# End of the experts: the last down weights in column halves, squares between them, the residual kept in its own order

## The chip, the cores and the metric

The kernel runs on one core of a Trainium2 chip. The metric is the device time of one execution in microseconds (us), the median of several runs. In the program and the profile TensorE is PE (its weight loads PEld), VectorE is DVE, ScalarE is ACT, GpSimd is POOL and the engine that issues most transfers is SP.

## What is computed

Two transformer blocks, one after the other, on 256 tokens of width 1024. The first block is a mixer (attention and convolution) and then a mixture of 32 experts with top 2 of one group of 8; the second is a block with an LRU, attention and an MLP. The change sits at the seam of the two: the end of the experts, the norm of their sum, and the first norm of the second block.

```python
    a = jnp.einsum('nd,edf->nef', t, w_gate)
    b = jnp.einsum('nd,edf->nef', t, w_up)
    hid = jax.nn.silu(a) * b * combine[:, :, None]
    routed = jnp.einsum('nef,efd->nd', hid, w_down)
    shared = (jax.nn.silu(t @ w_sh_gate) * (t @ w_sh_up)) @ w_sh_down
    return (routed + shared).reshape(bsz, slen, d)
...
        h = h + rms_norm(ffn, post_ffn_norm[l])
...
        h = rmsnorm(x, norm_mix_g[l])
        proj = h @ w_in[l]
```

`rms_norm(x, g)` divides x by the root of the mean of its squares over the 1024 columns (plus 1e-6) and multiplies by g. All is float32.

## The kernel before

Each engine has its own program, written by hand in order; semaphores join them. The weights stream through a ring of slots of 1 MB each (`slot(s)`, 12 in the experts, 8 in the second block). The 32 experts are worked in 8 quads of 4 (`q` from 0 to 7). A quad uses slots 0 to 3 for w_gate, 4 to 7 for w_up, 8 to 11 for w_down. SP issues the loads of the even slots and POOL those of the odd ones (`expert_slabs`), each as soon as the quad before has used the slot.

On PE a quad is: 64 passes of gate (`gate_or_up`, L2162), 64 of up (L2162), two transposes of the hidden rows (`turn_hidden`, L2169), down (`down`, L2176: 128 rows by 1024 columns into banks 2 and 3), and combine (L2183): the rows, copied from PSUM to `yrow` by ACT (columns 0 to 511, L889) and DVE (512 to 1023, L1516), are multiplied by the transposed selection `sel_T` and added to the tokens' sums in banks 4 to 7. A token tile t (128 tokens, two of them) has banks 4+2t and 5+2t. In the last quad combine of quad 6 comes between gate and up, followed by 16 filler matmuls (`keep_busy`, L2076).

After the last combine: PE takes a branch on `overflow` (L2288, L2289) around a long block that serves experts with over 32 tokens and that is not entered here, then issues 6 fillers, waits for the first tile of the sum (`h_ffn`), issues 8 more, and transposes the normed tiles (`turn_rows`, L2087) ahead of the first unit of the second block (L1843 to L1845, 24 passes for each unit). ACT and DVE do for each token tile: square with a sum (L930), root (L933), reciprocal (L1604), sum times root times gain from PSUM (L1605), plus the residual (L1609), square (L937), root, reciprocal (L1614), scale (L1615); then the high and low parts XH and XL of the transposed tiles. The residual is `h_tok`, which holds its columns in another order: `by_row` reads a row with steps of 128 elements, and `in_order` names the same columns in natural order. Between these, ACT splits the first units of new weights into a high part (`high2`, L648) and DVE into a low part (`low2`, L1133). ACT loads the table of roots ahead of the first square (`square_root_ahead`, L656).

Of the kernel before, what the change touches and what calls it, by code (L numbers as in the profile page):

```python
# [12 lines left out]
ALU = mybir.AluOpType  # L13
# [108 lines left out]
def build(nc, A, out):  # L122

    ctx = ExitStack()
    with ctx:
# [7 lines left out]
        def const(name):  # L133
# [5 lines left out]
                    "overflow_known", "lambda_abs", "ple_root"),  # L139
            scalar=("meta_std", "router_high", "mix_std", "group_exp", "pair_exp", "lambda_exp"),  # L140
            tensor=("angles", "kpe_swapped", "mix_sums", "routed", "ranks", "expert_totals"))
# [112 lines left out]
        gain_ffn = ar(0, D)  # L254

# [161 lines left out]

        def expert_slabs(queue, parity):

            for q in range(QUADS):  # L420
                for s in range(parity, RING, 2):
# [13 lines left out]
        def _(sp):  # L435
# [33 lines left out]
            expert_slabs(sp, 0)  # L469

# [45 lines left out]
        def _(pool):  # L516
# [70 lines left out]
            pool.dma_start(gain_mix, broadcast(A["post_mix_norm"][0])).then_inc(ev("gain_mix_loaded"), 16)  # L587
# [7 lines left out]
            pool.dma_start(gain_ffn, broadcast(A["post_ffn_norm"][0])).then_inc(ev("gain_ffn_loaded"), 16)  # L595
# [23 lines left out]
            for gain, name in ((gain_mlp, "norm_mlp_g_2"), (gain_ple, "norm_ple_g_2"), (gain_final, "norm_final_g_2")):  # L619
                v = A[name] if name == "norm_final_g_2" else A[name][0]  # L620
                pool.dma_start(gain, broadcast(v)).then_inc(ev("gains_loaded"), 16)
# [5 lines left out]
        def _(act):  # L627
# [186 lines left out]
            junk2 = junk.rearrange("p (b n) -> p b n", b=2)  # L814
# [69 lines left out]
            def rows_of(q):  # L884

                act.wait_ge(ev("expert_slab_used"), (q + 1) * RING)
# [15 lines left out]
            for q in range(1, QUADS):  # L902
# [3 lines left out]
                silu_of(q)  # L906
                if q % 2 == 0:
                    turned_weights(o)
                rows_of(q)
                if q == 4:  # L910
                    act.wait_ge(*mark("lambda_abs"))
                    s.activation(small_lru[:, 2 * DC:3 * DC], small_lru[:, DC:2 * DC], ACT.Exp)\
                        .then_inc(ev("scalar_mark"), 1)
            act.wait_ge(*mark("overflow_known"))
            more = act.value_load(overflow[0:1, 0:1], min_val=0, max_val=1)
            with act.If(more > 0):
# [7 lines left out]
                act.wait_ge(*by_tensor("combined", (ROUNDS - 1) * QUADS - 1))  # L924

            high2(0)
            square_root_ahead(1)
            for t in range(TT):
                act.wait_ge(ev("ffn_summed"), t + 1)
                s.activation(junk2, ps[:, 4 + 2 * t:6 + 2 * t, :], ACT.Square, accum_out=st(6, t))\  # L930
                    .then_inc(ev("tok_square"), 1)
                act.wait_ge(ev("tok_square"), 2 * TT + t + 1)
                s.activation(st(7, t), st(6, t), ACT.Sqrt, scale=1.0 / D, bias=EPS).then_inc(ev("tok_std"), 1)  # L933
            high2(1)
            for t in range(TT):
# [4 lines left out]
                if t == 0:  # L940
# [1623 lines left out]
```

## Time and profile before

| | us |
|---|---|
| median of 3 runs | 899.44 (898.21 to 900.03) |
| the profiled execution, its own time | 899.61 |
| its span, first to last instruction | 897.9 |
| PE busy in the span | 811.9 |
| DVE busy | 485.1 |
| ACT busy | 381.3 |

The span is what the trace shows; 1.7 us of the execution's time lie around it. Times of rows are counted from the span's start. The experts end and the second block begins near 385 to 401 us.

### The profile page before, as it was taken

The page shows a single profiled execution, that of the slowest core. Times are in us where ns is not written, and L with a number is a line of the kernel's source. Part 1 is how long each engine was busy: PE and PEld are TensorE (multiplying, and loading weights), DVE is VectorE, ACT ScalarE, POOL GpSimd, SP SyncE. Part 2 cuts the span into 40 slices and gives each one's busy share as a digit, 9 for nine tenths or more (in the row PEclk, how much of TensorE's full clock was granted, in tenths as well). Part 3 has the DMA queues.
Part 4 walks back from the last instruction along what each step waited for, and adds up shares of the span by engine and source line. Part 5 has one row for each costly group of instructions (what it writes and reads, how often), then busy time and mean ns, then how long its engine had stood idle before and what let it go on. Part 6 is the DMA issues. An engine that isn't in the chain of part 4 may idle for free.

```text
span 897.9 us, 13410 instructions
## 1 busy us (share of the span) xinstructions
PE 811.9 (90%) x5491; PEld 642.5 (72%) x5491; DVE 485.1 (54%) x799; ACT 381.3 (42%) x643; POOL 48.4 (5%) x114
## 2 busy tenths in 40 slices
PE   6989999997877676879999998999999999999995
PEld 5977879764444332449989885558888999999974
DVE  6786648411110030064936585776666666666675
ACT  5564558310000100065456845655444544444454
POOL 5000030101010001000000000000000000000000
PEclk9998999999897888899999998999999999999998
DMA  9951154899999999996418554127555555555101
GB/s 281 376 194 47 48 217 182 346 380 423 420 420 422 420 421 421 411 344 210 141 63 313 189 197 142 48 97 255 165 166 177 188 188 187 189 186 195 49 1 47
DMA packets 76974, 205.81 MB, mean 229 GB/s; under 512 B 5720, under 2 KB 48896, under 8 KB 64624
## 3 DMA queue, kind: packets, MB, share of 16 engines
q1 hardware_dynamic: 68430, 150.44, 47.2%
q0 software_dynamic: 8480, 54.49, 15.0%
q8 instruction: 45, 0.74, 0.3%
q14 instruction: 17, 0.14, 0.0%
q10 hardware_dynamic: 2, 0.00, 0.0%
HBM read 203.87 MB, written 1.05 MB: 228 GB/s over the span
## 4 chain that ended last, share of the span: by engine, by line
PE 71%; DMA 16%; DVE 6%; ACT 4%; issue 2%; SPq 0%; POOL 0%; ACTq 0%; DVEq 0%
DMA big<-in_w_up 13%; PE ps L2049 10%; PE ps L2050 10%; PE ps L2051 9%; PE ps L1843 9%; PE ps L1845 8%; PE ps L1844 8%; PE ps L2162 5%; DMA big<-in_w_down 3%; PE ps L2141 1%; PE ps L2176 1%; DVE WL L1133 1%; PE ps L2396 1%; ACT WH L648 1%; PE ps L2333 1%
## 5 line engine op out<-in xcount | busy, mean ns | idle before, releaser
L1133 DVE TENSOR_TENSOR WL<-big,WH 128x1024 fp32r<-128x1024 f32 x154 | 186.6, 1222 | 105.9 <-ACT WH L648 105.0
L648 ACT ACTIVATE WH<-big 128x1024 fp32r<-128x1024 f32 x154 | 160.5, 1054 | 70.5 <-PE ps L2051 70.0
L1843 PE MATMUL ps<-XH,WH 128*128 128x256 f32 (+1 forms) x640 | 187.6, 293 | 2.1 <-DVE XL L1198 0.9
L1845 PE MATMUL ps<-XH,WL 128*128 128x256 f32 (+1 forms) x640 | 183.3, 286 | 0.0
L1844 PE MATMUL ps<-XL,WH 128*128 128x256 f32 (+1 forms) x640 | 183.3, 286 | 0.0
L1843 PEld LDWEIGHTS ps<-XH,WH 128*128 128x128 f32 x640 | 123.9, 194 | 7.8 <-issue 5.0
L1844 PEld LDWEIGHTS ps<-XL,WH 128*128 128x128 f32 x640 | 124.0, 194 | 0.8
L1845 PEld LDWEIGHTS ps<-XH,WL 128*128 128x128 f32 x640 | 123.8, 193 | 0.0
L2162 PE MATMUL ps<-big 128*32 128x256 f32 x1024 | 77.6, 470 | 40.8 <-DMA big<-in_w_gate 25.2
L2049 PE MATMUL ps<-WH,XH 128*128 128x512 f32 x240 | 98.0, 408 | 1.8 <-ACT big L986 1.0
L2162 PEld LDWEIGHTS ps<-big 128*32 128x32 f32 x1024 | 42.5, 134 | 76.9 <-issue 66.3
L2050 PE MATMUL ps<-WH,XL 128*128 128x512 f32 x240 | 94.1, 392 | 0.0
L2051 PE MATMUL ps<-WL,XH 128*128 128x512 f32 x240 | 94.1, 392 | 0.0
L1504 DVE TENSOR_TENSOR big<-big,ps 128x256 f32<-128x256 f32 x8 | 3.4, 421 | 124.9 <-ACT big L882 124.8
L2049 PE MATMUL ps<-WH,HH 128*128 128x512 f32 x152 | 59.9, 394 | 0.6 <-DVE HL L1798 0.6
L2050 PE MATMUL ps<-WH,HL 128*128 128x512 f32 x152 | 59.4, 391 | 0.0
L2051 PE MATMUL ps<-WL,HH 128*128 128x512 f32 x152 | 59.2, 390 | 0.0
L2049 PEld LDWEIGHTS ps<-WH,XH 128*128 128x128 f32 x240 | 45.3, 189 | 13.5 <-issue 2.8
L1125 DVE TENSOR_TENSOR WL<-big,WH 128x1024 fp32r<-128x1024 f32 (+1 forms) x39 | 40.5, 1044 | 25.6 <-ACT WH L639 25.4
L2051 PEld LDWEIGHTS ps<-WL,XH 128*128 128x128 f32 x240 | 45.3, 189 | 9.8
L2050 PEld LDWEIGHTS ps<-WH,XL 128*128 128x128 f32 x240 | 45.4, 189 | 7.8
L1075 ACT ACTIVATE HH<-big 128x256 fp32r<-128x256 f32 x32 | 13.4, 418 | 76.1 <-DVE big L1795 76.1
(397 smaller groups left out, 1085.2 us busy)
## 6 DMA issues: line engine op xcount, KB each, us to landing
big<-in_w_in SPq DMA_DIRECT2D x35, 1024.0 KB, 9.4
big<-in_w_gate SPq DMA_DIRECT2D x16, 1024.0 KB, 14.6
big<-in_w_up SPq DMA_DIRECT2D x16, 1024.0 KB, 15.0
big<-in_w_gate POOLq DMA_DIRECT2D x16, 1024.0 KB, 18.7
big<-in_w_up POOLq DMA_DIRECT2D x16, 1024.0 KB, 19.2
big<-in_w_down SPq DMA_DIRECT2D x16, 1024.0 KB, 15.4
big<-in_w_down POOLq DMA_DIRECT2D x16, 1024.0 KB, 19.4
big<-in_w_mlp_up SPq DMA_DIRECT2D x16, 1024.0 KB, 5.4
```

The source lines that it names most:

```text
L648: s.activation(dst, src, ACT.Copy).then_inc(ev("unit_high"), 1)
L1075: s.activation(HH[:, f % 2, :], zx[:, f % 2, :], ACT.Copy).then_inc(ev("relu_high"), 1)
L1125: v.tensor_tensor(dst, src, h.bitcast(F32), ALU.subtract).then_inc(ev("unit_split"), 1)
L1133: v.tensor_tensor(dst, src, h.bitcast(F32), ALU.subtract).then_inc(ev("unit_split"), 1)
L1843: mm(o, h, rh, start=first, stop=False, skip_group_check=skip)
L1844: mm(o, h, rl, start=False, stop=False, skip_group_check=skip)
L1845: return mm(o, l, rh, start=False, stop=last, skip_group_check=skip)
L2049: mm(o, h, WH[:, b, w], start=first, stop=False, skip_group_check=skip)
L2050: mm(o, l, WH[:, b, w], start=False, stop=False, skip_group_check=skip)
L2051: return mm(o, h, WL[:, b, w], start=False, stop=last, skip_group_check=skip)
L2141: last = mm(o, h_tok[:, t, c * P:(c + 1) * P], sel[:, b, t, first:first + width].bitcast(F32), start=t == 0, stop=t == TT - 1)
L2162: last = mm(ps[j * CAP:(j + 1) * CAP, 1, up * FF:(up + 1) * FF], x(c)[:, j * CAP:(j + 1) * CAP], slot(first_slot + j)[:, c * FF:(c + 1) * FF],
```

## The change

It does six things, all at the end of the last quad. The four last w_down slabs are loaded in two column halves each (0 to 511, 512 to 1023); SP loads slots 8, 9 and 10 (all first halves, then all second), POOL slot 11, and SP starts the second block's weights only once POOL's second half is in. PE does down for the first half into bank 2, combine for it, then down for the second half in two quarters into banks 3 and 0, and combine for it. ACT squares the first half's sums while the second goes on. The residual, scaled and in natural order, is copied by ACT to slot 7 ahead of the last rows (so the load of the second block's slab 7 waits for `h_ffn`). DVE multiplies the sums by the gain (`weighted`) ahead of the root, so that one operation after the root adds the residual. The root's table is loaded after the last silu, and the splits of the first units of new weights are placed later.

```diff
+        weighted = lambda t: ar((1 + t) * D, D)
+        residual = lambda t: slot(RING2 - 1)[:, t * D:(t + 1) * D]
...
+        def last_down_halves(queue, slots):
+            for n in range(2):
+                for s in slots:
+                    queue.wait_ge(ev("expert_slab_used"), (QUADS - 2) * RING + s + 1)
...
+                    cols = slice(n * 512, (n + 1) * 512)
+                    queue.dma_start(slot(s).rearrange("p (c n) -> p c n", c=2)[:, :, cols], w[:, :, cols])\
+                        .then_inc(*last_half(n, s))
...
             expert_slabs(sp, 0)
+            last_down_halves(sp, (8, 9, 10))
+            sp.wait_ge(ev("last_half_by_pool"), 16)
...
             for m in range(RING2):
                 sp.wait_ge(ev("expert_slab_used"), RING * (QUADS - 1) + m + 1)
+                if m == RING2 - 1:
+                    sp.wait_ge(ev("h_ffn"), TT)
                 second_slab(m)
...
             expert_slabs(pool, 1)
+            last_down_halves(pool, (11,))
# ACT
                 silu_of(q)
+                if q == QUADS - 1:
+                    square_root_ahead(1)
...
+                if q == QUADS - 1:
+                    for t in range(TT):
+                        ins = s.activation(in_order(residual(t)), by_row(h_tok[:, t, :]), ACT.Copy, scale=st(4, t))
+                    ins.then_inc(ev("scalar_mark"), 1)
                 rows_of(q)
...
+            act.wait_ge(*mark("half_combined"))
+            square_part(0, 0, half_square[:, 0:1])
+            square_part(0, 1, half_square[:, 1:2]).then_inc(ev("scalar_mark"), 1)
+            act.wait_ge(ev("expert_slab_used"), QUADS * RING)
+            s.activation(yrow[:, 768:D], ps[:, 0, 0:256], ACT.Copy).then_inc(ev("rows_by_scalar"), 1)
...
-            high2(0)
-            square_root_ahead(1)
             for t in range(TT):
                 act.wait_ge(ev("ffn_summed"), t + 1)
-                s.activation(junk2, ps[:, 4 + 2 * t:6 + 2 * t, :], ACT.Square, accum_out=st(6, t))\
+                square_part(1, t, st(6, t)).then_inc(ev("tok_square"), 1)
...
+            high2(0)
             high2(1)
# DVE
-            low2(0)
...
+            for t in range(TT):
+                dve.wait_ge(ev("tok_square"), 2 * TT + t + 1)
+                chain(scale_part(1, t))
                 dve.wait_ge(ev("tok_std"), 2 * TT + t + 1)
                 chain(v.reciprocal(st(8, t), st(7, t)))
...
-                v.scalar_tensor_tensor(out=in_order(ffn_tmp[:, t, :]), in0=by_row(h_tok[:, t, :]), scalar=st(4, t),
-                                       in1=in_order(ffn_tmp[:, t, :]), op0=ALU.mult, op1=ALU.add)\
-                    .then_inc(ev("h_ffn"), 1)
+                v.scalar_tensor_tensor(out=ffn_tmp[:, t, :], in0=weighted(t), scalar=st(8, t), in1=residual(t),
+                                       op0=ALU.mult, op1=ALU.add).then_inc(ev("h_ffn"), 1)
...
                 v.tensor_scalar(h2n[:, t, :], ffn_tmp[:, t, :], st(11, t), None, ALU.mult).then_inc(ev("tok_normed"), 1)
-            low2(1)
+                low2(t)
# PE
+            last_down(2, 0, 512).then_inc(ev("tensor_mark"), 1)
             pe.wait_ge(ev("rows_by_scalar"), QUADS)
+            for t in range(TT):
+                last = combine(sel_T[:, 1, 1], t, (0,))
+            last.then_inc(ev("tensor_mark"), 1)
+            pe.wait_ge(ev("last_halves"), 16 * (QUAD - 1))
+            pe.wait_ge(ev("last_half_by_pool"), 16)
+            last_down(3, 512, 768)
+            last_down(0, 768, D).then_inc(ev("expert_slab_used"), QUAD)
+            pe.wait_ge(ev("rows_by_scalar"), QUADS + 1)
             pe.wait_ge(ev("rows_by_vector"), QUADS)
             for t in range(TT):
-                combine(sel_T[:, 1, 1], t).then_inc(ev("ffn_summed"), 1)
+                combine(sel_T[:, 1, 1], t, (1,)).then_inc(ev("ffn_summed"), 1)
```

On PE, from the up matmuls of the last quad to the branch and past it, the order before is (`ps` is PSUM, `big` the arena with slots and rows):

```order
L2162 MATMUL ps<-big 32x256 x32
L2169 MATMUL ps<-ident,big 128x128 x2
L2176 MATMUL ps<-big 32x512 x16
L2183 MATMUL ps<-big 128x512 x4
L2288 TENSOR_LOAD overflow
L2288 ISA x2
L2289 COMPARE_AND_BRANCH
```

and in the changed kernel, same place:

```order
L2225 MATMUL ps<-big 32x256 x32
L2232 MATMUL ps<-ident,big 128x128 x2
L2352 MATMUL ps<-big 32x512 x8
L2246 MATMUL ps<-big 128x512 x2
L2352 MATMUL ps<-big 32x256 x16
L2246 MATMUL ps<-big 128x512 x2
L2374 TENSOR_LOAD overflow
L2374 ISA x2
L2375 COMPARE_AND_BRANCH
```

Down and combine are cut in two and interleaved; the branch stays behind the last combine, and behind the skipped block the 14 fillers and 16 transposes stay as they were.

On ACT, from the last silu (first row) to the branch, the order of the changed kernel is (L940 copies the residual, L916 and L956 the rows, L950 squares):

```order
L909 ACTIVATE big<-ps 128x256
L684 ACT_TABLE_LOAD
L684 ACTIVATE warm<-ones 1x1
L940 ACTIVATE big<-hT,stat 128x1024 x2
L916 ACTIVATE big<-ps 128x512
L950 ACTIVATE big<-ps 128x512 x2
L956 ACTIVATE big<-ps 128x256
L958 TENSOR_LOAD overflow
```

Before, the copy of the rows (L889) followed the silu (L882) directly and was the last before the branch; the table load and the two copies of 128x1024 now stand between them, ahead of the rows for which PE waits.

On DVE, behind the skipped block, the order before is:

```order
L1133 TENSOR_TENSOR WL<-big,WH 128x1024
L1604 RECIPROCAL stat<-stat 128x1
L1605 SCALAR_TENSOR_TENSOR big<-ps,stat,big 128x1024
L1609 SCALAR_TENSOR_TENSOR big<-hT,stat,big 128x1024
L1604 RECIPROCAL stat<-stat 128x1
L1605 SCALAR_TENSOR_TENSOR big<-ps,stat,big 128x1024
L1609 SCALAR_TENSOR_TENSOR big<-hT,stat,big 128x1024
L1614 RECIPROCAL stat<-stat 128x1
L1615 TENSOR_SCALAR big<-big,stat 128x1024
L1614 RECIPROCAL stat<-stat 128x1
L1615 TENSOR_SCALAR big<-big,stat 128x1024
L1133 TENSOR_TENSOR WL<-big,WH 128x1024
```

and in the changed kernel (L1568 is sum times gain for one half, L1673 the addition of the residual, L1180 `low2`):

```order
L1568 TENSOR_TENSOR big<-ps,big 128x512
L1672 RECIPROCAL stat<-stat 128x1
L1673 SCALAR_TENSOR_TENSOR big<-big,stat 128x1024
L1568 TENSOR_TENSOR big<-ps,big 128x512
L1672 RECIPROCAL stat<-stat 128x1
L1673 SCALAR_TENSOR_TENSOR big<-big,stat 128x1024
L1677 RECIPROCAL stat<-stat 128x1
L1678 TENSOR_SCALAR big<-big,stat 128x1024
L1180 TENSOR_TENSOR WL<-big,WH 128x1024
L1677 RECIPROCAL stat<-stat 128x1
L1678 TENSOR_SCALAR big<-big,stat 128x1024
L1180 TENSOR_TENSOR WL<-big,WH 128x1024
```

The two operations of 128x1024 for each tile are one of 128x512 and one of 128x1024, and the first split of weights has moved from ahead of both tiles to between the two scalings.

## Rows read from the trace of the kernel before

**Rows 1.** The chain that ended last, 350 to 425 us: start, duration, what.

```profile
357.21 23.88 DMA big<-in_w_down
381.23 3.67 PE ps L2176 x32
```

**Rows 2.** The same chain, 384 to 402 us; ACTq is ACT's sequencer.

```profile
385.68 0.05 ACTq L916
...
387.00 1.28 ACT L656
...
394.74 2.07 DVE big L1609
...
396.83 1.16 ACT big L937 x2
...
398.45 0.75 DVE big L1615
399.20 1.13 DVE WL L1133
...
400.88 0.36 PE ps L1843
```

**Rows 3.** Timeline of PE, 366 to 420 us: start, busy, operation, count, idle before.

```profile
371.25 4.22 PE L2076 MATMUL ps<-router 128*128 128x512 f32 x16
...
375.40 3.66 PE L2162 MATMUL ps<-big 128*32 128x256 f32 x64
...
381.23 3.64 PE L2176 MATMUL ps<-big 128*32 128x512 f32 x32 [0.64 <-DMA big<-in_w_down]
...
385.76 3.67 PE L2183 MATMUL ps<-big 128*128 128x512 f32 x8 [0.90 <-DVE big L1516]
...
393.37 5.06 PE L2076 MATMUL ps<-router 128*128 128x512 f32 x14 [3.93 <-issue]
...
398.26 2.09 PE L2087 MATMUL ps<-ident,big 128*128 128x128 f32 x16
```

**Rows 4.** Source line L2289: PE's branch (ns min/median/max, first and last start).

```profile
L2289 PEldq COMPARE_BRANCH  x1: 6646/6646/6646, 386.7 to 386.7; - x1
```

**Rows 5.** Windows: length, busy (count) of PE, PEld, DVE, ACT, POOL; clock; DMA.

```profile
393.00:396.00 3.00, 2.63 (x9) 2.13 (x10) 2.93 (x4) 2.31 (x4) 0.00 (x0) 0.78 1.10 348
396.00:398.00 2.00, 2.00 (x7) 1.52 (x6) 1.62 (x3) 1.15 (x2) 0.00 (x0) 0.50 1.10 350
...
410.00:420.00 10.00, 10.00 (x86) 10.00 (x85) 3.73 (x4) 6.20 (x9) 0.00 (x0) 1.00 0.67 215
```

**Rows 6.** Groups of ACT and of DVE by form: busy us, mean ns of one, idle before.

```profile
L648 ACT ACTIVATE WH<-big 128x1024 fp32r<-128x1024 f32 x154 | 160.5, 1054 | 70.5 <-PE ps L2051 70.0 <-issue 0.4
...
L889 ACT ACTIVATE big<-ps 128x512 f32<-128x512 f32 x8 | 4.8, 597 | 65.9 <-PE ps L2176 65.9
L844 ACT ACTIVATE hT<-big,stat 128x1024 f32<-128x1024 f32 x2 | 4.1, 2180 | 0.0
...
L1609 DVE SCALAR_TENSOR_TENSOR big<-hT,stat,big 128x1024 f32<-128x1024 f32 x2 | 4.0, 2018 | 0.1
...
L1370 DVE SCALAR_TENSOR_TENSOR big<-big,stat,hT 128x1024 f32<-128x1024 f32 x2 | 2.6, 1285 | 0.1
```

**Rows 7.** Timeline of ACT, 379 to 403 us.

```profile
379.13 0.38 ACT L882 ACTIVATE big<-ps 128x256 f32<-128x256 f32 x1 [22.10 <-PE ps L2162]
...
389.30 0.18 ACT L930 ACTIVATION_READ_ACCUMULATOR big<-ps 128x1 f32 x1
```

**Rows 8.** POOL's last w_down transfer, issued at 357.2 us: KB, us to landing.

```profile
big<-in_w_down POOLq DMA_DIRECT2D x1, 1024.0 KB, 23.9
```

**Rows 9.** DMA queues, 376 to 378 us (q0 POOL's, q1 SP's): packets, MB, share.

```profile
q0 software_dynamic: 98, 0.69, 83.1%
q1 hardware_dynamic: 92, 0.11, 15.4%
```

More of the change, by code:

```diff
@@ L416, in expert_slab, with last_half @@
             queue.dma_start(dst, src).then_inc(ev(expert_in(s)), 16)
+        def last_half(n, s):
+            if s == RING - 1:
+                return ev("last_half_by_pool" if n else expert_in(s)), 16
+            return ev("last_halves" if n else expert_in(s) if s % 2 == 0 else "last_slot_9"), 16
+        def last_down_halves(queue, slots):
+            for n in range(2):
+                for s in slots:
+                    queue.wait_ge(ev("expert_slab_used"), (QUADS - 2) * RING + s + 1)
+                    w = A["w_down"][0][bass.ds((QUADS - 1) * QUAD + s % QUAD, 1)].rearrange("e (p c) n -> p (e c) n", p=P)
+                    cols = slice(n * 512, (n + 1) * 512)
+                    queue.dma_start(slot(s).rearrange("p (c n) -> p c n", c=2)[:, :, cols], w[:, :, cols])\
+                        .then_inc(*last_half(n, s))
         def expert_slabs(queue, parity):
             for q in range(QUADS):
-                for s in range(parity, RING, 2):
+                for s in range(parity, RING if q < QUADS - 1 else 2 * QUAD, 2):
                     if q == 0:
@@ L620, in _ @@
                 v = A[name] if name == "norm_final_g_2" else A[name][0]
-                pool.dma_start(gain, broadcast(v)).then_inc(ev("gains_loaded"), 16)
+                pool.dma_start(gain, broadcast(v)).then_inc(ev("rows_loaded"), 16)
         @block.scalar
@@ L1568, in _ @@
                     softplus_of_lambda()
+            dve.wait_ge(*loaded("gain_ffn"))
+            for t in range(TT):
+                ins = scale_part(0, t)
+            chain(ins)
             dve.wait_ge(*mark("overflow_known"))
@@ L2179, in down, with combine @@
                 return last
-            def combine(weights, t):
-                for n in range(2):
+            def combine(weights, t, halves_=(0, 1)):
+                for n in halves_:
                     last = mm(ps[:, 4 + 2 * t + n, :], weights[:, t * P:(t + 1) * P], yrow[:, n * 512:(n + 1) * 512],
@@ L2280, in _, with last_down @@
                     pe.wait_ge(ev("sel_T_ready"), o + 1)
-                wait_slots(q, 2 * QUAD)
-                down(2 * QUAD).then_inc(ev("expert_slab_used"), QUAD)
-            pe.wait_ge(ev("rows_by_scalar"), QUADS)
+                if q < QUADS - 1:
+                    wait_slots(q, 2 * QUAD)
+                    down(2 * QUAD).then_inc(ev("expert_slab_used"), QUAD)
+            def last_down(bank, a, b):
+                for f in range(2):
+                    for j in range(QUAD):
+                        last = mm(ps[j * CAP:(j + 1) * CAP, bank, 0:b - a], hidT[:, f, j * CAP:(j + 1) * CAP],
+                                  slot(2 * QUAD + j)[:, f * D + a:f * D + b],
+                                  start=f == 0, stop=f == 1, skip_group_check=True)
+                return last
+            for s in (8, 10, 11):
+                pe.wait_ge(*slab_e(QUADS - 1, s))
+            pe.wait_ge(ev("last_slot_9"), 16)
+            last_down(2, 0, 512).then_inc(ev("tensor_mark"), 1)
+            pe.wait_ge(ev("rows_by_scalar"), QUADS)
+            for t in range(TT):
+                last = combine(sel_T[:, 1, 1], t, (0,))
[5 more added lines that the diff above has]
+            pe.wait_ge(ev("rows_by_scalar"), QUADS + 1)
             pe.wait_ge(ev("rows_by_vector"), QUADS)
             for t in range(TT):
-                combine(sel_T[:, 1, 1], t).then_inc(ev("ffn_summed"), 1)
+                combine(sel_T[:, 1, 1], t, (1,)).then_inc(ev("ffn_summed"), 1)
             more = pe.value_load(overflow[0:1, 0:1], min_val=0, max_val=1)
```

56 lines of the change are left out of this document (37 added, 19 removed).

## The prediction

> **What bounds the kernel now.** I read the page first, then the chain of waits around the seam, then the timelines of PE, ACT and DVE there. The chain says that the last w_down slab holds the end of the experts: 23.88 us on a transfer, down from 381.23 [rows 1], and then a ladder of ACT and DVE steps up to 400.88, where the first unit of the second block starts on PE [rows 2]. From there PE is busy without a break, 10.00 of the 10 us from 410 [rows 5], so I let a shift of that start pass to the end one for one. So the question is only: when does the first unit start?
>
> Two paths reach it, and the chain shows one of them. The other is PE's own program. After the last combine PE sits idle for 3.93 us ("issue"), then runs 14 fillers to 398.26, and only then transposes [rows 3]. The idle time is its branch: it starts at 386.7, 0.9 us behind the start of combine, and holds for 6.65 us [rows 4], where ACT's branch on the same word takes 0.05 [rows 2]. The transposes of the first tile begin as soon as the fillers end. So the ladder of ACT and DVE and the ladder of PE arrive together: from the start of the transposes, 398.26, PE alone would have needed some 2.35 us to the first unit (8 transposes, half of the 2.09 us of the 16, then a pair, ACT's high and DVE's low part at 0.4 to 0.5 each), so 400.6 against 400.88. **PE has 0.3 us of slack there.** What makes its last combine end later makes the kernel slower, whatever is saved on ACT and DVE.
>
> **The change, step by step.**
>
> Loads. The total is the same; SP's queue has 3 MB and POOL's 1 MB in place of 2 and 2. Before, the last slab landed 23.9 us behind its issue, at 381.1 [rows 1, 8]. Where POOL's large packets met SP's small ones of w_in, POOL moved 0.69 MB and SP 0.11 in 2 us at about the same number of packets [rows 9]: the queues take turns by packet. Halves have pieces of 2 KB in place of 8, so SP's first halves advance slowly while POOL finishes its up slab, then evenly. I put the first halves at 379 to 381 and the second ones at 382.5 to 384.5 (an estimate: the 381.1 of before with the same bytes, plus the gain row's 0.5 MB, which now moves in between, at 350 GB/s [rows 5], and up to two more for smaller pieces). The hidden rows are ready at 381.2 as before, since up starts at 375.40 behind the fillers [rows 3], so first halves cost nothing up to 381.2 and, by the next step, up to some 383 unseen. The second halves are wanted at 387.5. w_in then follows: its first slab, 1 MB at those 350 GB/s, lands 3 us later, near 387; it is split at 393, as shown below. Cost of all this: 0; cover 3 us and more.
>
> Down, first half: 16 of 32 passes, half of 3.67 us, ends at 383.2 [rows 1].
>
> ACT's way to the rows. Silu ends at 379.5 [rows 7], table load 1.28 [rows 2] and the warm-up operation to 380.9, then two copies of the residual with steps of 128 elements. No row has ACT *reading* so. Below: the plain copy, 1.05 us (L648). Above: ACT *writing* such a pattern, 2.18 (L844). DVE reading this very pattern takes 2.02 against 1.29 for the same operation on plain rows (L1609, L1370) [rows 6]. Both nearest rows pay for the pattern, so I take 2.1 each: ACT is free at 385.1. At 1.05 it is free at 383.0, and the rows start at 383.2. The Trainium skill (SBUF — State Buffer, section "Door 1: The DMA port swizzle", its note on cachelines) says that fp32 strides over 4 elements leave full bandwidth; by it too the copies cost double and the sum is the one below, but no run here shows an ACT read of that kind.
>
> The rows' copy, 0.60 [rows 6], and 0.1 to PE: combine of the first half starts at 385.8, just where the whole combine started before (385.76 [rows 3]). So nothing of the overlap is left: PE idles 2.6 us between the halves, and now still has the second down ahead.
>
> PE from 385.8: four passes of combine 1.8 (half of 3.67); second down, 32 passes of 256 columns in place of 16 of 512, 1.8 (half of the 3.66 of 64 such passes [rows 3]), to where its readers start 2.0, so 389.6; DVE's copy of 256 columns 0.4 (an estimate, two thirds of ACT's 0.60 for 512), 0.1 to PE, so combine starts at 390.1; four passes and the drain 2.0: **the last combine ends at 392.1, against 389.43 before** (385.76 plus 3.67), +2.7. The passes cost in sum what they did. But behind 385.8 there stood one combine, and now stand half a combine, half a down, a copy and the other half combine.
>
> ACT and DVE meanwhile. Squares of the first half (two times 0.6 and 0.18 [rows 6, 7]) fit under the second down. From the sum of tile 0 at 391.3: square of 512 columns and its sum 0.8; gain times sum on DVE 0.7; reciprocal and gap 0.2; one addition 1.29 on plain rows: tile 0 at 394.3. Tile 1: another 2.3, at 396.6, where L1609 ended at 396.8 before [rows 2]. All that DVE saves (0.7 a tile by plain rows, 0.6 by a half product, the table load) is spent on starting 3 us later. Then both splits on ACT (2.1) lie ahead of the square of tile 0, so squares end at 396.6 and 398.0 and root 0.2 behind each; DVE scales tile 0 to 397.8, splits a unit (1.13), scales tile 1 to 400.0, splits again to 401.1, low part: first unit at 401.8 by this path (399.20 to 400.88 is the same last stretch [rows 2]). So this path alone gives +0.9. With quick residual copies it would be 399.9, so -1.0.
>
> PE's branch. Its 6.65 us can hang on two things. If it waits for the last matmul (idle 3.93 behind it [rows 3]), the fillers start at 392.1 + 3.9 = 396.0, +2.7. If it is a fixed time from where it is reached (0.9 behind the start of combine, 390.1 + 0.9 + 6.65), they start at 397.7, +4.3. The Trainium skill (Runtime: NRT & Kernel Launch, section "Instruction fetch mechanics") says that a taken branch whose target is outside the two pages at hand stalls for a fetch; the 6.65 us agree with that, and by it a target within those pages would make the short branch of the rivals below. I take the first, as the two halves of combine leave less queued work behind which a fixed wait could hide, and it is the smaller claim; the second stays in the range.
>
> Fillers. From their start to the first transpose went 4.9 us (393.37 to 398.26), with the granted clock at 0.78 and then 0.50, which is 1.2 GHz [rows 3, 5]. At the full 2.4 GHz 14 take 3.7, by the 16 at 371.25 in 4.22 [rows 3]. PE is idle before them as long as it was, so I keep 4.9: transposes from 400.9, first unit 2.35 later. Bounds -1.4 (no drop) and +1.5 (half clock for all).
>
> **Sum.** +2.7 on the last combine, minus the 0.3 of slack: first unit at 403.3 in place of 400.88, **+2.4 us**. 899.61 for this profile would be 902.0; on the median, 0.17 below it, 901.8. A difference under 0.2% (1.8 us) can't be told from none.
>
> **Rivals.**
> - Branch of fixed length: +4.1, 903.5. For it: the branch is reached ahead of the last passes. Against: nothing in the trace says what it waits for.
> - One more drop of the clock, in the new idle stretch 383.2 to 385.8 or over all fillers: +1.5 to 1.7 on the forecast, 903.4. For it: an idle stretch of 3.9 us was followed by a drop; the new one is 2.6 us, so open.
> - Quick residual copies (1.05 each): rows at 383.2, all 1.9 earlier, +0.5, 899.9. Decides from a copy under some 1.15 us; at 1.6 each half of it.
> - Not slower, by a short branch: if it costs PE what it costs ACT, fillers start right behind the last combine and PE's path is no bound; then the path of ACT and DVE stands, +0.9 with slow copies (900.3) and -1.0 with quick ones (898.4). It decides once PE sits idle behind the last combine for 3.3 us or less in place of 3.93 (that is within 0.2%), and in full at 2.4. Against: the skipped block is the same and PE's code ahead of it grew by only 16 passes.
> - The halves don't overlap at all because the transfers are late: from 383.2 on each us costs one. Little speaks for it.
>
> **How the numbers follow.** Forecast 0.40 (901.8, own range 900.6 to 903.2), fixed branch 0.22, extra clock drop 0.13, quick copies 0.15, short branch 0.08, late loads or others 0.02. Slower by over 0.2%: most of the first three, 0.65. Within: quick copies, short branch with slow copies and the low edge of the forecast, 0.28. Faster: short branch and quick copies together with a clock that stays up, or something that I don't see, 0.07. The range 899.6 to 904.6 leaves out about one in ten on either side.
>
> **What would show it.** In the changed profile: the two residual copies at 2.0 to 2.2 us each and the copy of the first rows behind them at 385; PE idle 2 to 3 us between first down and first combine; last combine ending near 392; a branch row and the fillers near 396 (397.7 for the rival); transposes at 400 or later with no wait for the normed tile; first unit at 403. I am wrong if the fillers start before 394.5, if the copies are near 1 us, or if the transposes wait for DVE.

## The result and the profile after

The changed kernel takes 902.91 us (median of 14 runs, 899.6 to 906.87) against 898.18 for the kernel before (14 runs, 897.64 to 900.03): ratio 1.0054, 95% interval 1.004 to 1.0067. It is slower by about 4.7 us. The profiled execution took 901.96, its span is 900.2.

The chain that ended last in the changed kernel, around the seam (start, duration, what):

```profile
378.43 1.28 ACT L684
...
379.93 3.94 ACT big L940 x2
383.87 0.49 ACT big L916
384.40 1.98 PE ps L2246 x4
...
390.84 5.59 issue
396.43 5.15 PE ps L2139 x14
...
402.71 0.48 ACT XH L991
```

In [rows 2] ACT and DVE filled the chain up to the first unit. Here they fill it only ahead of the first combine, where PE waits for the table load and the two residual copies. From 384.40 on the chain is PE's own, but for DVE's copy of the last rows (0.44) and a step each of ACT and DVE ahead of the first unit, and its largest piece is idle time. PE's timeline for the same stretch (start, busy, operation, count, idle before and its releaser), which answers to [rows 3]:

```profile
380.02 1.92 PE L2352 MATMUL ps<-big 128*32 128x512 f32 x16 [0.52 <-DVE big L1556]
384.40 1.98 PE L2246 MATMUL ps<-big 128*128 128x512 f32 x4 [2.46 <-ACT big L916]
386.32 1.93 PE L2352 MATMUL ps<-big 128*32 128x256 f32 x32
388.89 1.96 PE L2246 MATMUL ps<-big 128*128 128x512 f32 x4 [0.64 <-DVE big L1564]
396.43 5.15 PE L2139 MATMUL ps<-router 128*128 128x512 f32 x14 [5.59 <-issue]
401.42 1.91 PE L2150 MATMUL ps<-ident,big 128*128 128x128 f32 x16
403.85 0.36 PE L1906 MATMUL ps<-XH,WH 128*128 128x256 f32 x1 [0.52 <-DVE XL L1682]
```

The first down waits for the hidden rows (L1556), not for a transfer. The last combine ends at 390.84 and the transposes need no wait for a normed tile. PE's branch, which answers to [rows 4], and the two residual copies (ns min/median/max, then first and last start):

```profile
L2375 PEldq COMPARE_BRANCH  x1: 6602/6602/6602, 389.8 to 389.8; - x1
L940 ACT ACTIVATE big<-hT,stat x2: 1996/2065/2134, 379.8 to 381.9; 128x1024 f32<-128x1024 f32 x2
```

And the last rows of DVE and of ACT on the other path, by their timelines (L1180 is DVE's last split, the other two are the low and high parts of the transposed tiles):

```profile
398.67 1.22 DVE L1180 TENSOR_TENSOR WL<-big,WH 128x1024 fp32r<-128x1024 f32 x1
403.22 3.23 DVE L1682 SCALAR_TENSOR_TENSOR XL<-ps,vec,XH 128x256 fp32r<-128x256 f32 x8 [3.33 <-ACT XH L991]
402.71 3.03 ACT L991 ACTIVATE XH<-ps,vec 128x256 fp32r<-128x256 f32 x8 [4.45 <-PE ps L2150]
```

DVE is done with everything at 399.9 and sits idle for 3.33 us, ACT for 4.45. The steps that were made shorter on them now end in front of a PE that comes late.

**A gauge.** The start of the first down wanders between profiles, 379 to 385 us, and PE waits 5.4 to 7.6 us for the last quad's gate weights in all of them; the stretch from the first unit to the end is 497.0 us before and 496.4 after. So I compare the stretch from the start of the last quad's down to the first unit, cut at three points of PE's timeline: A from down to the start of the last group of combine, B from there to the fillers, C from the fillers to the transposes, D from the transposes to the first unit. What happens ahead of this down, the gauge doesn't see.

| kernel | A | B | C | D | sum |
|---|---|---|---|---|---|
| before | 4.53 | 7.61 | 4.89 | 2.62 | 19.65 |
| changed | 8.87 | 7.54 | 4.99 | 2.43 | 23.83 |
| e1 | 4.55 | 3.10 | 8.86 | 3.17 | 19.68 |
| e2 | 10.52 | 1.39 | 6.54 | 3.61 | 22.06 |
| e3 | 8.86 | 7.53 | 2.73 | 2.99 | 22.11 |
| e4 | 7.13 | 7.56 | 5.80 | 2.43 | 22.92 |
| e5 | 6.23 | 7.63 | 4.85 | 2.64 | 21.35 |
| e6 | 5.97 | 7.55 | 4.90 | 2.70 | 21.12 |
| e7 | 8.98 | 7.56 | 5.02 | 2.42 | 23.98 |
| e8 | 7.13 | 1.39 | 7.98 | 3.23 | 19.73 |
| e9 | 8.76 | 7.71 | 4.87 | 2.42 | 23.76 |
| e10 | 4.45 | 7.57 | 4.91 | 2.70 | 19.63 |
| e11 | 9.01 | 1.39 | 6.54 | 3.61 | 20.55 |
| e12 | 7.13 | 1.39 | 6.53 | 3.62 | 18.67 |

The change adds 4.2 us, all of it in A. The table also shows at once what B is: 7.5 to 7.7 wherever the branch stands behind combine, whether the group of combine ahead of it has 8 passes (3.67 to 3.70 us: before, e5, e6, e10) or 4 (1.96: changed, e3, e4, e7, e9). It is 0.9 to the branch and 6.6 in it. The changed kernel, e7 and e9 have the same order of work behind down and lie at 23.76 to 23.98, so a difference under 0.2 says nothing here.

### The profile page after: what moved, and what is told of

Its sections match the earlier page's. It is cut to its first block, busy times and chain, and to the rows that moved or that the text cites. A ratio compares the mean times of both kernels' runs of the same rounds, so it can differ in the third digit from the quotient of the medians.

```text
span 900.2 us, 13463 instructions
## 1 busy us (share of the span) xinstructions
PE 808.0 (90%) x5507; PEld 640.7 (71%) x5507; DVE 483.5 (54%) x802; ACT 386.3 (43%) x650; POOL 48.8 (5%) x114
## 4 chain that ended last, share of the span: by engine, by line
PE 72%; DMA 15%; DVE 5%; ACT 4%; issue 3%; SPq 0%; POOL 0%; ACTq 0%; DVEq 0%
DMA big<-in_w_gate 15%; PE ps L2112 10%; PE ps L2113 9%; PE ps L2114 9%; PE ps L1906 9%; PE ps L1907 8%; PE ps L1908 8%; PE ps L2225 5%; PE ps L2139 2%; PE ps L2204 1%; DVE WL L1180 1%; PE ps L2246 1%; PE ps L2482 1%; PE ps L2419 1%; PE ps L2468 1%
## 5 line engine op out<-in xcount | busy, mean ns | idle before, releaser
L1180 DVE TENSOR_TENSOR WL<-big,WH 128x1024 fp32r<-128x1024 f32 x154 | 186.6, 1222 | 104.4 <-ACT WH L676 103.5
L2225 PE MATMUL ps<-big 128*32 128x256 f32 x1024 | 74.7, 456 | 43.7 <-DMA big<-in_w_gate 28.3
```

The lines of the kernel that those rows point to most:

```text
L1180: v.tensor_tensor(dst, src, h.bitcast(F32), ALU.subtract).then_inc(ev("unit_split"), 1)
L2225: last = mm(ps[j * CAP:(j + 1) * CAP, 1, up * FF:(up + 1) * FF], x(c)[:, j * CAP:(j + 1) * CAP], slot(first_slot + j)[:, c * FF:(c + 1) * FF],
```

## Experiments

The expectations name three theories of what makes the changed kernel slower: theory 1 (T1), PE's own path, with a later last combine, then a branch of fixed length, then 14 fillers; theory 2 (T2), the ladder of ACT and DVE; theory 3 (T3), the loads. Each run has its own median of the kernel before, taken beside it.

**e1: the kernel before, PE's branch moved ahead of the last quad.** The code of the last quad stands twice, once in the block that is skipped and once behind it, so that the jump is over before the quad's first matmul (row of its branch: 6.05 us from 357.3, while PE waits for gate weights).

```diff
+            for q in range(1, QUADS - 1):
+                quad_of(q)
...
             with pe.If(more > 0):
+                end_of_experts()
...
+            with pe.If(more < 1):
+                end_of_experts()
```

> The kernel before, with PE's branch around the overflow block taken ahead of the last quad, where PE waits for w_gate anyway (the last quad's code stands in both arms). Theory 1 (PE's own path sets the first unit of the second block: last combine, then a branch of a fixed 6.6 us from where it is reached, then 14 fillers): before, that path had 0.3 us of slack, so taking the branch out of it gains nothing more than that: 898.2 less 0 to 0.5. Theory 2 (the ladder of ACT and DVE sets it): the same, 898.2. Both: the idle time of 3.9 us behind the last combine is gone, and PE waits for the normed tile instead.

Measured: 899.37 us (12 runs, 897.04 to 902.8) against 898.83, ratio 1.001 (0.9997 to 1.0024). PE's timeline:

```profile
392.33 1.95 PE L2076 MATMUL ps<-router 128*128 128x512 f32 x6
396.85 3.29 PE L2076 MATMUL ps<-router 128*128 128x512 f32 x8 [2.57 <-DVE big L1609]
401.19 1.09 PE L2087 MATMUL ps<-ident,big 128*128 128x128 f32 x8 [1.04 <-DVE big L1615]
```

The idle time behind combine is gone and nothing is gained: PE now waits for DVE at each step. The ladder alone takes 19.68, the kernel before 19.65; PE's path alone, with the ladder shortened, takes 19.63 (e10). In the kernel before, the two paths met, closer than the gauge can tell.

**e2: the changed kernel with the same edit.** The wrapper is e1's, around the last quad with its halves.

```diff
             with pe.If(more > 0):
+                end_of_experts()
...
+            with pe.If(more < 1):
+                end_of_experts()
```

> The changed kernel with the same early branch. Theory 1: the fillers start right behind the last combine (391 in place of 396.4), the transposes wait for DVE, first unit at about 400.5 in place of 403.9: -3.3, 899.6 on the median, and the wide scatter of the changed kernel (899.6 to 906.9) shrinks, since PE is no longer idle for 5.6 us. Theory 2: no change, 902.9. Theory 3 (the transfers or the held-back weights are what costs): no change, 902.9.

Measured: 901.97 us (11 runs, 900.63 to 904.03), ratio 1.0035 (1.0018 to 1.0051), 22.06 us in the stretch. Theory 1 had expected 899.6. B fell from 7.5 to 1.4, but A grew by 1.65. PE's timeline, and the windows (length, busy and count of PE, PEld, DVE, ACT, POOL, then clock, DMA):

```profile
386.05 2.56 PE L2246 MATMUL ps<-big 128*128 128x512 f32 x4 [2.46 <-ACT big L916]
388.54 2.99 PE L2358 MATMUL ps<-big 128*32 128x256 f32 x32
392.18 1.96 PE L2246 MATMUL ps<-big 128*128 128x512 f32 x4 [0.65 <-DVE big L1564]
...
400.11 1.09 PE L2150 MATMUL ps<-ident,big 128*128 128x128 f32 x8 [0.88 <-DVE big L1678]
```

```profile
383.70:387.30 3.60, 1.25 (x3) 0.68 (x4) 0.00 (x0) 2.29 (x2) 0.00 (x0) 1.00 1.10 349
387.30:390.70 3.40, 3.40 (x26) 1.02 (x28) 0.17 (x1) 1.26 (x4) 0.00 (x0) 0.50 1.10 348
```

Behind the idle stretch ahead of the first combine the granted clock stood at 0.50, 1.2 GHz, for 3.4 us, and combine and the second down took 2.56 and 2.99 in place of 1.98 and 1.93. Without that (e11) the stretch is 20.55. So within the stretch the branch was worth 3.3 us to the changed kernel (23.83 to 20.55; 3.4 from e7, which has the same fillers in the gap) and nothing to the kernel before.

The early branch has a price of its own ahead of the stretch. In the chains of the changed kernel and of e12, the last w_gate slab that PE waits for:

```profile
337.36 23.53 DMA big<-in_w_gate
```

```profile
336.65 24.91 DMA big<-in_w_gate
```

In the five profiles with an early branch (e1, e2, e8, e11, e12) this transfer takes 24.2 to 24.9 us, in eight with a late one 23.0 to 23.6 (the chain of the kernel before doesn't show it). From the start of quad 6's down to its combine, behind the last quad's gate, it is 16.1 to 16.4 us against 15.3 to 15.9, on average 0.7 more. Why the transfer takes longer, no run shows. The medians agree with it without proving it: e1, level with the kernel before in the stretch, lies 0.5 us above it, with no difference still inside the interval.

**e3: the changed kernel with 6 fillers in place of 14.**

```diff
             pe.wait_ge(ev("h_ffn"), 1)
-            keep_busy(8, 0)
             turn_rows(h2n, 1)
```

> The changed kernel with 6 fillers in place of 14 behind the branch. Theory 1: the transposes come 8 fillers earlier, 3.4 us at the half clock, of which DVE's path (first unit not before 400.5) lets 2.5 to 3.3 count: about 900.2; less if the missing fillers keep the clock at 1.2 GHz into the first units. Theories 2 and 3: no change.

Measured: 900.92 us (12 runs, 898.81 to 906.4), ratio 1.0031 (1.0009 to 1.0052), 22.11 us in the stretch; 900.2 was expected.

```profile
397.50 2.93 PE L2139 MATMUL ps<-router 128*128 128x512 f32 x6 [5.57 <-issue]
400.23 2.47 PE L2150 MATMUL ps<-ident,big 128*128 128x128 f32 x16
```

Fewer fillers bring the first unit forward by 1.7 us. They save 2.3 in C; 0.6 went back in D, in slower transposes and the pair behind them. Fillers lie on the path that sets the end, as T1 says; by T2, dropping them would have gained nothing. The medians (902.91 and 900.92, against 898.18 and 898.83 before) go the same way, with intervals that overlap.

**e4: the residual copied without its reordering** (it leaves out the reordering, so the residual's columns are mixed).

```diff
-                        ins = s.activation(in_order(residual(t)), by_row(h_tok[:, t, :]), ACT.Copy, scale=st(4, t))
+                        ins = s.activation(residual(t), h_tok[:, t, :], ACT.Copy, scale=st(4, t))
```

> The changed kernel with the residual copied by ACT without the change of order (it leaves out the reordering, so the values are others). The copies should take 1.05 us each in place of 2.0. Theory 1: first rows, both combines, the branch and all behind them come 1.7 to 1.9 us earlier: 901.1. Theory 2: the same 1.8 through the ladder. Theory 3: nothing.

Measured: 901.48 us (9 runs, 899.84 to 906.03), ratio 1.0043 (1.0024 to 1.0062), 22.92 in the stretch.

```profile
381.76 1.98 PE L2246 MATMUL ps<-big 128*128 128x512 f32 x4 [0.72 <-ACT big L916]
...
393.81 5.96 PE L2139 MATMUL ps<-router 128*128 128x512 f32 x14 [5.61 <-issue]
```

The first combine starts 2.64 us behind down in place of 4.38, so the pattern costs 1.7 us on PE's path; the two copies took 1.13 us each. Of that 0.8 was lost again over the fillers (C 5.80 in place of 4.99), which ran at half clock almost to their end (granted 0.50 from 394 to 398 us, 0.71 over the next two).

**e5: the kernel before with the new loads alone.** PE does down as a whole and waits for all halves.

```diff
             expert_slabs(sp, 0)
+            last_down_halves(sp, (8, 9, 10))
+            sp.wait_ge(ev("last_half_by_pool"), 16)
...
+                    pe.wait_ge(ev("last_halves"), 16 * (QUAD - 1))
+                    pe.wait_ge(ev("last_half_by_pool"), 16)
                 down(2 * QUAD).then_inc(ev("expert_slab_used"), QUAD)
```

> The kernel before with nothing but the loads of the change: last w_down slabs in column halves, three on SP and one on POOL, the second block's weights held until POOL's second half is in; PE waits for all of them and does down whole. Theory 1 (PE's path behind the first down costs the time): 898.8 within 0.2%, since down waits for the hidden rows and the slabs land within a microsecond or two of them. Theory 3 (the loads cost it): 902 or more, with first down later than 1 us behind the hidden rows.

Measured: 901.69 us (5 runs, 901.02 to 904.16) against 898.49, ratio 1.0047 (1.0033 to 1.0061). Not what I expected.

```profile
381.34 5.34 PE L2195 MATMUL ps<-big 128*32 128x512 f32 x32 [3.21 <-DMA big<-in_w_down]
387.57 3.67 PE L2202 MATMUL ps<-big 128*128 128x512 f32 x8 [0.90 <-DVE big L1535]
```

PE waits for the last half 2.7 us longer than for the hidden rows (3.21 of idle time, where the changed kernel has 0.52), and behind it down ran at half clock for most of its length (granted 0.50 from 382 to 384 us; 5.34 in place of 3.64). The gauge begins behind that wait and shows only the second part, 1.7. New loads do cost something, then, in a kernel that wants all halves at once. Whether the changed kernel does, e9 tells.

**e6: the changed kernel with down and combine whole again on PE** (new loads kept).

```diff
-            last_down(2, 0, 512).then_inc(ev("tensor_mark"), 1)
-            pe.wait_ge(ev("rows_by_scalar"), QUADS)
-            for t in range(TT):
-                last = combine(sel_T[:, 1, 1], t, (0,))
-            last.then_inc(ev("tensor_mark"), 1)
             pe.wait_ge(ev("last_halves"), 16 * (QUAD - 1))
             pe.wait_ge(ev("last_half_by_pool"), 16)
+            last_down(2, 0, 512).then_inc(ev("tensor_mark"), 1)
...
+            for t in range(TT):
+                last = combine(sel_T[:, 1, 1], t, (0,))
```

> The changed kernel with down and combine whole on PE (both halves of down, then the rows, then combine of all columns; ACT squares the first half's sums behind it), all else as changed. From the start of the last down: combine ends at +8.7 us (before +8.2, changed +10.8), branch of 6.6 from +5.8, fillers at +12.4 (before +12.1, changed +16.4), first unit at +20.0 (before 19.7, changed 23.8). Theory 1: some 3.8 us below the changed kernel, 899.2, the same as before. Theory 2 (ladder) and 3 (loads): 902 to 903 as changed.

Measured: 901.75 us (9 runs, 899.2 to 903.96), ratio 1.0029 (1.0012 to 1.0047), 21.12 us in the stretch. Theory 1 had expected 899.2 and 20.0 in the stretch. Something else confounds it: down took 5.35 us behind 2.99 of waiting for w_down, as in e5. It tells nothing of the halves alone; e10 repeats it with the old loads.

**e7: the changed kernel with 10 fillers in the gap ahead of the first combine.**

```diff
             last_down(2, 0, 512).then_inc(ev("tensor_mark"), 1)
+            keep_busy(10, 1)
             pe.wait_ge(ev("rows_by_scalar"), QUADS)
```

> The changed kernel with 10 fillers on PE in the 2.5 us in which it waits for the first rows. If a drop of the clock in that gap, as seen in the early-branch run at 387 to 391, makes the upper part of the changed kernel's scatter, then runs of 904 to 907 become rare and the median falls by 0 to 1.5 us: 901.5 to 902.9. If not, the same scatter and median. The branch and the order are untouched, so theory 1 has it stay above 901.

Measured: 902.14 us (5 runs, 900.87 to 903.36), ratio 1.0043 (1.003 to 1.0056), 23.98 us in the stretch. The fillers (2.60 us) all but fit into the wait of 2.46 and cost 0.1. The runs lie closer together (900.87 to 903.36) than the changed kernel's 899.6 to 906.87, but five runs don't settle that.

**e8: early branch, residual copied a quad earlier, first splits ahead of the second squares.** The residual goes to the arena's first rows at q = 6, when ACT waits for gate weights anyway; the gain row gives way to it and is loaded later, and the weighted sums move to slot 7.

```diff
-        residual = lambda t: slot(RING2 - 1)[:, t * D:(t + 1) * D]
+        residual = lambda t: ar(t * D, D)
...
+                rows_of(q)
+                if q == QUADS - 2:
...
-                rows_of(q)
...
+            high2(0)
             act.wait_ge(*mark("half_mean"))
...
+            low2(0)
             dve.wait_ge(*mark("residual_kept"))
```

> The changed kernel with three edits: PE's branch ahead of the last quad, the residual copied in quad 6 into a buffer that is free by then, and the first split of new weights ahead of the second half's squares (ACT and DVE idle there). Theory 1: first rows 2.1 us behind the start of down, last combine ends at +9.1, fillers at full clock behind it, then the ladder of ACT and DVE is the bound: first unit at +18.3 where before has 19.7, so 897.4, 0.15% under the kernel before. Theory 3: 902.

Measured: 898.46 us (12 runs, 897.25 to 903.73) against 898.49, ratio 1.0005 (0.9985 to 1.0024), 19.73 us in the stretch. The slowdown is gone, though 897.4 was expected. The splits cost: ahead of the second group of fillers PE sits idle for 2.67 us, where e12, without them, has 1.60.

```profile
393.72 3.52 PE L2142 MATMUL ps<-router 128*128 128x512 f32 x8 [2.67 <-DVE big L1675]
```

**e9: the changed kernel with the old loads** (whole slabs, POOL and SP two each).

```diff
-                for s in range(parity, RING if q < QUADS - 1 else 2 * QUAD, 2):
+                for s in range(parity, RING, 2):
...
-            last_down_halves(sp, (8, 9, 10))
-            sp.wait_ge(ev("last_half_by_pool"), 16)
```

> The changed kernel with the loads of before (whole w_down slabs, two on SP and two on POOL, the second block's weights not held); PE's halves and all else as changed. Theory 1 (PE's path behind the first down): the first down waits for whole slabs, 0 to 0.5 us later than changed, and the stretch from first down to first unit stays at 23.8 us: 902.9 to 903.4. Theory 3 (the loads cost the time, as they did in the kernel before with the new loads, +3.2): 899.7.

Measured: 903.09 us (12 runs from 901.17; one took 1032.53, the median isn't moved by it) against 898.25, ratio 1.0048 (1.0032 to 1.0063), 23.76 us in the stretch, against 23.83 with the new loads. They cost the changed kernel nothing: its second down starts at 386.32 without a wait. T3 falls.

**e10: e9 with down and combine whole on PE.** All edits of ACT and DVE stay but the order of two rows; loads are those of before, and down (still in 48 passes, but 3.65 us long) and combine each run in one piece.

```diff
+            act.wait_ge(ev("expert_slab_used"), QUADS * RING)
+            s.activation(yrow[:, 768:D], ps[:, 0, 0:256], ACT.Copy).then_inc(ev("rows_by_scalar"), 1)
             act.wait_ge(*mark("half_combined"))
...
-            act.wait_ge(ev("expert_slab_used"), QUADS * RING)
-            s.activation(yrow[:, 768:D], ps[:, 0, 0:256], ACT.Copy).then_inc(ev("rows_by_scalar"), 1)
```

> The changed kernel with old loads and with down and combine whole: only the ladder of ACT and DVE, the residual and the table load are as changed. The run with whole down on the new loads had its down wait 2 us for the second halves and fall to the half clock, so it told nothing of theory 1. Theory 1: last combine ends 8.7 us behind the start of down (before 8.2), branch 6.6, fillers at +12.4, first unit at +20.0 (before 19.7, changed 23.8): 898.8 to 899.2, the same as before. Theory 2 (the ladder costs it): 901 or more.

Measured: 898.0 us (12 runs, 896.74 to 903.29) against 898.25, ratio 1.0 (0.9979 to 1.0021), 19.63 us in the stretch. PE's timeline, and its branch:

```profile
379.97 3.65 PE L2349 MATMUL ps<-big 128*32 128x512 f32 x48 [0.85 <-DMA big<-in_w_down]
384.42 3.70 PE L2243 MATMUL ps<-big 128*128 128x512 f32 x8 [0.81 <-ACT big L950]
391.99 5.07 PE L2136 MATMUL ps<-router 128*128 128x512 f32 x14 [3.87 <-issue]
396.90 2.17 PE L2147 MATMUL ps<-ident,big 128*128 128x128 f32 x16
```

```profile
L2367 PEldq COMPARE_BRANCH  x1: 6605/6605/6605, 385.3 to 385.3; - x1
```

The last combine starts 4.45 us behind down, as before. The table load and both residual copies now run beside the whole down and cost nothing, and the shorter steps of DVE gain nothing. From e9 to e10 only the halves go, and 4.1 us with them: the halves are the cause, in a kernel whose residual copies stand ahead of the rows and whose branch stands behind the last combine. e12 keeps the halves and moves those two, and is not slower either.

**e11: e2 with e7's fillers in the gap.**

```diff
                 last_down(2, 0, 512).then_inc(ev("tensor_mark"), 1)
+                keep_busy(10, 1)
                 pe.wait_ge(ev("rows_by_scalar"), QUADS)
```

> The early branch of the second run together with 10 fillers in the gap between first down and first combine. In that run the clock fell to half at 387.3 to 390.7, so combine and the second down took 1.65 us longer, and only 1.8 of the expected 3.3 us came back. Theory 1: with the gap filled the clock stays up, first unit 20.4 us behind first down (changed 23.8, early branch alone 22.1): 899.6. If it stays at 22 with a full clock, something else on the way costs 1.7 us.

Measured: 900.38 us (12 runs, 899.44 to 903.89) against 898.25, ratio 1.0023 (1.0009 to 1.0036), 20.55 us in the stretch.

```profile
381.44 2.57 PE L2139 MATMUL ps<-router 128*128 128x512 f32 x10
384.10 1.98 PE L2246 MATMUL ps<-big 128*128 128x512 f32 x4
...
396.52 1.09 PE L2150 MATMUL ps<-ident,big 128*128 128x128 f32 x8 [0.87 <-DVE big L1678]
398.51 1.65 PE L2150 MATMUL ps<-ident,big 128*128 128x128 f32 x8 [0.90 <-DVE big L1678]
```

With the branch away and the clock kept up to 398.9, what is left of the slowdown is 0.9 us in the stretch, and it is the ladder of ACT and DVE, for which PE now waits. Then the second transposes and the first unit ran at half clock (granted 0.50 from 398.9 to 402.2), and from the first unit to the end this profile took 498.3 us where the changed kernel took 496.4. That, and the 0.7 us ahead of the stretch, may be why the median is 0.8 above what I expected.

**e12: e2 with the residual copied a quad earlier** (e8 without its splits).

```diff
+                rows_of(q)
+                if q == QUADS - 2:
...
-                rows_of(q)
```

> The changed kernel with two edits: PE's branch ahead of the last quad, and the residual copied in quad 6 into a free buffer. The splits of new weights stay where the change put them (the run that had the first split ahead of the squares lost 1.4 us on DVE there: its first gain product of the second half began at 391.5, not 390.0). Theory 1: rows 2.1 us behind the start of down, last combine at +9.1, then the ladder: first unit at +18.4 (before 19.7): 897.5. Theory 2 and 3: 899 or more.

Measured: 898.41 us (12 runs, 897.29 to 902.39) against 898.25, ratio 1.0 (0.9985 to 1.0014), 18.67 us in the stretch.

```profile
382.49 1.98 PE L2247 MATMUL ps<-big 128*128 128x512 f32 x4 [0.72 <-ACT big L917]
...
391.92 2.10 PE L2140 MATMUL ps<-router 128*128 128x512 f32 x8 [1.60 <-DVE big L1674]
394.90 1.09 PE L2151 MATMUL ps<-ident,big 128*128 128x128 f32 x8 [0.88 <-DVE big L1679]
```

This is the shortest stretch of all, 1.0 us under before, with a profiled execution of 897.29. The medians don't show it, and 897.5 was expected: some 0.7 of the 1.0 us goes ahead of the stretch, where the early branch has its price, and the rest is far under what they resolve. Against e8, which has the first splits ahead of the second squares, it is 1.06 shorter. No version beats the kernel before by more than can be measured.

## Why the prediction was right, and where it was off

**The path.** The forecast said that what makes PE's last combine end later makes the kernel slower, whatever is saved on ACT and DVE. The trace after and e9 with e10 bear that out: undo the halves and the time of before is back, undo the loads and nothing moves.

**The 0.3 us of slack.** Worked out as a pair of 400.6 and 400.88. e1 removed PE's idle time and the stretch stayed as it was, 19.68 against 19.65; e10 shortened the ladder and it stayed too, 19.63. The two paths did arrive together, and if there was slack, it was less than the 0.2 us that the gauge can tell.

**Loads at nothing.** Right for this kernel (e9). The second halves were put at 382.5 to 384.5, 1.4 to 3.4 us later than the last slab of before. In e5 the last of them was there at 381.1, but that profile ran 2.7 us ahead (down of quad 6 at 350.05, against 352.72 before), so by the clock of before it is 383.8, and the estimate held. What I then expected of e5 was wrong: in the prediction the hidden rows hid the first halves only, and a kernel that waits for all is exposed by the 2.7 us that e5 shows, and by 1.7 more of down at half clock.

**ACT's way to the rows.** 2.1 us was taken for a residual copy, by the nearest rows; the two took 2.0 and 2.13. Plain copies (e4) took 1.13 and started combine 1.7 us earlier. The Trainium skill (SBUF — State Buffer, section "Door 1: The DMA port swizzle", its note on cachelines) says that an access which crosses to a new line pays, and now e4 shows it for an ACT read. It gives no price for such a copy; the doubling that the prediction drew from it came from the neighbouring rows.

**The last combine.** Forecast 10.9 us behind the start of down (381.2 to 392.1), measured 10.82 (380.02 to 390.84). Behind the first down stand two hand-overs in place of one: 2.46 idle ahead of the first combine and 0.64 ahead of the last, where before had 0.90.

**The branch: the term that was mis-sized.** I took 3.9 us behind the last combine, tied to the last matmul, and named the fixed length as a rival with 22 in 100. It is the rival. In every one of nine traces with the branch behind combine, the branch starts 0.9 to 1.0 us behind the first pass of the last group and holds for 6.59 to 6.75 us, whether that group runs 3.67 us or 1.96. So with a shorter last group the idle time behind it grows, from 3.93 to 5.59: +1.7. It is 5.6 to 5.8 in all five with the short group, 3.9 to 4.0 in the four with the long one. The reason that I gave, "the smaller claim", was no evidence; the row of 6.65 us beside a combine still running for 2.7 us of it was, and I should have weighed it more. The Trainium skill (Runtime: NRT & Kernel Launch, section "Instruction fetch mechanics") says that a taken branch out of the two pages at hand waits for a fetch, which a length independent of the matmuls agrees with. A packet on the instruction queue does come in these traces, some 4 us behind the branch's start (last section), so a fetch may be part of it; that it is all of it, no run shows.

**Fillers and transposes.** 4.9 and 2.35 forecast, 4.99 and 2.43 measured. The granted clock was 0.52 over a longer stretch than before (windows of the changed kernel):

```profile
393.00:400.00 7.00, 3.57 (x8) 2.81 (x9) 6.75 (x10) 4.47 (x8) 0.00 (x0) 0.52 1.10 350
```

but the first half of it fell into idle time, and the fillers took as long as before, 5.15 against 5.06.

**The sum.** Forecast from down to first unit 22.1 (381.2 to 403.3), measured 23.83; the 1.7 between them is the branch. That the profiled execution was forecast at 902.0 and took 901.96 is luck: down started 1.2 us earlier than before and the rest of the kernel was 0.7 shorter. The stretch grew by 4.2 us where 2.4 were forecast, and 4.1 is what the rival of the fixed branch had. The medians differ by 4.7. The forecast of 901.8 also stood on 899.44, the median of three runs; from the 898.18 of fourteen, +2.4 would have been 900.6 and the rival's +4.1 would have been 902.3, with 902.91 measured. So the path, the direction and the size of the first term were right, and the branch was not.

**The path of ACT and DVE alone.** Put at +0.9, and at -1.0 with quick residual copies. Once the branch was out of the way it could be seen: e11 has +0.90, e12, with copies that no longer stand in front of the rows, -0.98. DVE's savings were real and were spent on a start that came later.

**One more drop of the clock.** It did not come in the changed kernel's profile, nor in those of e3 and e9, which have the same idle stretch; it came in e2's, at 1.65 us. Whether it is part of why the changed kernel's runs scatter over 7 us stays open: those of before lie within 2.4 beside them, but reach 903.79 among the 31 beside e1, so the scatter may not be the change's at all.

## What to carry to other kernels

Where two paths reach a point together, as here to within what the gauge can tell (0.2 us), shortening one gains nothing and lengthening the other costs all of it; so find the slack of the path that the chain does not show before pricing the one that it shows. Work cut in halves to overlap needs something to stand beside each half: count the hand-overs that come in, and what else the producer has in front of its first piece. A fixed wait is best placed where the engine is idle anyway: the same branch that cost the changed kernel 3.3 us behind the last combine cost 0.7 while PE waited for the last quad's weights. And a gauge over a short stretch needs a second one over what lies ahead of it, or such a price goes unseen.

## What the runs showed of the hardware

PE's taken branch over the skipped block held its sequencer for 6.59 to 6.75 us in all late positions and 6.03 to 6.49 in the early ones (e1, e2, e8, e11, e12), while the second, which isn't taken, since its block is entered, took 0.08:

```profile
L2384 PEldq COMPARE_BRANCH  x1: 6491/6491/6491, 354.2 to 354.2; - x1
L2414 PEldq COMPARE_BRANCH  x1: 80/80/80, 360.7 to 360.7; - x1
```

Matmuls issued ahead of it go on meanwhile: before, combine ran for 2.7 us of it. The DMA queue of instructions moved nothing in the 4.0 us after the branch of the changed kernel began (389.8 to 393.8), and one packet of 0.02 MB on the queue below (with one of 0.01 MB on a second) in the 2.7 us that follow:

```profile
q8 instruction: 1, 0.02, 2.7%
```

In the traces of before, e5, e6, e9 and e10 such a packet of 0.02 MB comes 3.5 to 4.5 us behind the branch's start too. So most of the 6.6 us passed before the transfer; what fills them no run here shows.

An ACT copy of 128x1024 that reads with steps of 128 elements takes 2.00 to 2.13 us (the changed kernel), where the same copy of plain rows takes 1.13 (e4).
